# Causal mask of the prompt attention added by TensorE, scores read in PSUM by VectorE and ScalarE

## The reference

```python
def mla_scores(q_lat, q_rope, ckv, krope):
    s = jnp.einsum('bthc,bsc->bhts', q_lat, ckv) + jnp.einsum('bthr,bsr->bhts', q_rope, krope)
    return s.astype(jnp.float32) * SM_SCALE

def mla_prompt(q_lat, q_rope, ckv, krope):
    ...
    def blk(i):
        start = i * Q_BLOCK
        ...
        s = mla_scores(ql, qr, ckv, krope)
        qpos = start + jnp.arange(Q_BLOCK)
        s = jnp.where(kpos[None, :] <= qpos[:, None], s, -jnp.inf)
        p = jax.nn.softmax(s, axis=-1).astype(ckv.dtype)
        return jnp.einsum('bhts,bsc->bthc', p, ckv)
```

## Time and profile before

| | |
|---|---|
| time, median of 3 runs | 1596.08 us (1591.57 to 1596.08) |
| the profiled execution's own time | 1595.94 us |
| its span | 1594.4 us |
| TensorE busy | 1478.6 us (93%) |
| VectorE busy | 694.9 us (44%) |
| ScalarE busy | 457.0 us (29%) |
| chain that ended last, by engine | TensorE 87%, VectorE 8%, DMA 2% |

### The profile page before, as it was taken

How to read it: one execution, slowest core, us unless ns; L and a number is a source line. 1 busy time by engine, 2 the same in 40 slices (tenths; PEclk the granted TensorE clock), 3 DMA queues, 4 the chain that set the end, 5 groups by cost and what they waited for, 6 DMA issues and landing times.

```text
span 1594.4 us, 30443 instructions
## 1 busy us (share of the span) xinstructions
PE 1478.6 (93%) x11990; PEld 1373.2 (86%) x11990; DVE 694.9 (44%) x1155; ACT 457.0 (29%) x774; POOL 144.7 (9%) x275
## 2 busy tenths in 40 slices
PE   5999999999688899999998899988789999999993
PEld 5999999999578888878788878767779999999993
DVE  5444444222565443444343445455474444442224
ACT  4222222222323232333332321223332222222220
POOL 0000000000030015353540000000000000000000
PEclk9999999999778999999999889997879999999996
DMA  3222222322064327575754222132312222223211
GB/s 125 91 92 81 90 92 87 107 91 86 14 233 144 113 81 207 168 206 160 209 162 153 92 93 92 57 109 93 123 42 91 91 81 91 91 90 101 88 67 57
DMA packets 80225, 173.06 MB, mean 109 GB/s; under 512 B 11961, under 2 KB 46778, under 8 KB 78458
## 3 DMA queue, kind: packets, MB, share of 16 engines
q1 hardware_dynamic: 69882, 150.68, 28.7%
q0 software_dynamic: 10240, 20.99, 4.6%
HBM read 157.55 MB, written 14.07 MB: 108 GB/s over the span
## 4 chain that ended last, share of the span: by engine, by line
PE 87%; DVE 8%; DMA 2%; issue 1%; ACT 1%; SPq 0%; DVEq 0%; ACTq 0%
PE acc L559 51%; PE acc L654 15%; PE acc L784 2%; PE acc L781 2%; PE bank_a L744 1%; PE bank_a L745 1%; PE bank_a L724 1%; PE bank_v L927 1%; PE bank_v L759 1%; PE bank_v L903 1%; PE acc L811 1%; PE bank_v L912 1%; DVE rpost L1441 1%; PE bank_a L607 1%; DVE x_lo L1425 1%
## 5 line engine op out<-in xcount | busy, mean ns | idle before, releaser
L559 PE MATMUL acc<-x_hi,w_hi 128*128 128x272 f32 x1536 | 323.5, 292 | 33.1 <-DVE x_lo L1425 29.6
L1400 DVE TENSOR_TENSOR w_lo<-w_raw,w_hi 128x1024 fp32r<-128x1024 f32 (+1 forms) x172 | 223.5, 1300 | 229.4 <-ACT w_hi L1014 225.7
L559 PE MATMUL acc<-x_hi,w_lo 128*128 128x272 f32 x1536 | 319.4, 290 | 0.0
L559 PE MATMUL acc<-x_lo,w_hi 128*128 128x272 f32 x1536 | 319.4, 290 | 0.0
L559 PEld LDWEIGHTS acc<-x_hi,w_hi 128*128 128x128 f32 x1536 | 242.8, 191 | 37.4 <-issue 23.7
L1014 ACT ACTIVATE w_hi<-w_raw 128x1024 fp32r<-128x1024 f32 (+1 forms) x172 | 190.9, 1110 | 199.5 <-PE acc L654 89.2
L559 PEld LDWEIGHTS acc<-x_lo,w_hi 128*128 128x128 f32 x1536 | 244.2, 191 | 0.0
L559 PEld LDWEIGHTS acc<-x_hi,w_lo 128*128 128x128 f32 x1536 | 242.8, 191 | 0.0
L654 PE MATMUL acc<-x_hi,w_hi 128*128 128x272 f32 x688 | 218.8, 318 | 16.2 <-DVE qk L1524 9.2
L654 PE MATMUL acc<-x_hi,w_lo 128*128 128x272 f32 x688 | 205.1, 298 | 0.0
L654 PE MATMUL acc<-x_lo,w_hi 128*128 128x272 f32 x688 | 204.7, 298 | 0.0
(11 more groups left out here) (267 smaller groups left out, 1540.1 us busy)
## 6 DMA issues: line engine op xcount, KB each, us to landing
w_raw<-in_w_gu SPq DMA_DIRECT2D x88, 512.0 KB, 3.4
w_raw<-in_w_dn SPq DMA_DIRECT2D x32, 704.0 KB, 4.0
w_raw<-in_w_in SPq DMA_DIRECT2D x44, 512.0 KB, 4.4
pg<-in_key_t POOLq DMA_DIRECT2D x128, 96.0 KB, 2.5
pg<-in_key_t SPq DMA_DIRECT2D x128, 96.0 KB, 2.2
pg<-in_lat POOLq DMA_DIRECT2D x128, 64.0 KB, 2.6
pg<-in_lat SPq DMA_DIRECT2D x128, 64.0 KB, 2.4
g_mid<-sq SPq DMA_DIRECT2D x16, 272.0 KB, 3.8
```

Of the source, the lines that this page charges most:

```text
L559: ins = nc.tensor.matmul(acc[pair][:, a, 0:HT], w[:, slot, n * P:(n + 1) * P], v[:, k, a * HT:(a + 1) * HT], start=first and n == 0 and te ...
L1400: nc.vector.tensor_tensor(wlo[:, slot, 0:tiles * P], raw[:, slot, 0:tiles * P], f32(whi[:, slot, 0:tiles * P]), ALU.subtract).then_inc(w_s ...
```

## The change

TensorE adds the mask to the scores with a third product in the same accumulation group: the identity matrix times the mask, 128 by 128, onto the last 128 columns of the block. VectorE takes the maximum straight from the PSUM bank, and ScalarE takes the exponential from the bank and writes it to `pr`. The copy `take` and VectorE's mask addition are gone. The bank is now freed by `expo`, which from the second head on also waits for the transposes of the head before, since it overwrites `pr`. In all three programs the dense call behind the scores, 18 products, is cut in two of 9, the first of which now stands between block 2 and block 3. VectorE does `normalise(h, 1)` before `highest(h, 3)`.

```diff
--- before.py
+++ after.py
@@ -310,7 +310,7 @@
         small_out = sem("small_out")
         g1_landed, g2_landed, g1_used, merged = sem("g1_landed"), [sem(f"g2_landed{i}") for i in range(2)], sem("g1_used"), sem("merged")
         pair_landed, qr_ready, qs_done = sem("pair_landed"), sem("qr_ready"), sem("qs_done")
-        mx_ready, ex_ready, inv_ready, pr_ready = sem("mx_ready"), sem("ex_ready"), sem("inv_ready"), sem("pr_ready")
+        mx_ready, pr_ready = sem("mx_ready"), sem("pr_ready")
         ptab_landed, wuv_landed = sem("ptab_landed"), sem("wuv_landed")
         pg_landed = [[[sem(f"pg_landed{w}{b}{q}") for q in range(4)] for b in range(2)] for w in ("sp", "pool")]
         pg_used = sem("pg_used")
@@ -743,7 +743,8 @@
                 b = bank_a(f"sc{h}{i}")
                 nc.tensor.matmul(b[:, 0:n], ql[:, e, i * P:n], ckvT[:, 0:n], start=True, stop=False)
                 nc.tensor.matmul(b[:, 0:n], qr[ROPE * e:ROPE * (e + 1), i * P:n], krT[ROPE * e:ROPE * (e + 1), 0:n],
-                                 start=False, stop=True).then_inc(a_ready, 1)
+                                 start=False, stop=False)
+                nc.tensor.matmul(b[:, i * P:n], ident, mask_qk, start=False, stop=True).then_inc(a_ready, 1)
 
             def turn(h, i):
 
@@ -845,8 +846,9 @@
                     scores(h, 1)
                     sample_scores(m0, (2, 3))
                     scores(h, 2)
+                    dense(9)
                     scores(h, 3)
-                    dense(18)
+                    dense(9)
                     sample_turn(m0)
                     turn(h, 0)
                     turn(h, 1)
@@ -1199,16 +1201,13 @@
             def piece(i):
                 return pr[:, PR_AT[i]:PR_AT[i] + (i + 1) * P]
 
-            def take(h, i):
-
-                act.wait_ge(a_ready, A.filled(f"sc{h}{i}"))
-                nc.scalar.activation(piece(i), A.bank(f"sc{h}{i}")[:, 0:(i + 1) * P], ACT.Copy).then_inc(a_read, 1)
-
             def expo(h, i):
 
                 act.wait_ge(mx_ready, 4 * h + i + 1)
-                nc.scalar.activation(piece(i), piece(i), ACT.Exp, scale=SM,
-                                     bias=sst[:, 4 + i:5 + i], accum_out=sst[:, 8 + i:9 + i]).then_inc(ex_ready, 1)
+                if h:
+                    act.wait_ge(a_ready, A.filled(f"tr{h - 1}{i}"))
+                nc.scalar.activation(piece(i), A.bank(f"sc{h}{i}")[:, 0:(i + 1) * P], ACT.Exp, scale=SM,
+                                     bias=sst[:, 4 + i:5 + i], accum_out=sst[:, 8 + i:9 + i]).then_inc(a_read, 1)
 
             def turned(h, i):
 
@@ -1256,16 +1255,13 @@
                     sample_new(PER * (p // 2))
                 for h in (2 * p, 2 * p + 1):
                     m0, m1 = step_of(2 * h), step_of(2 * h + 1)
-                    take(h, 0)
-                    take(h, 1)
                     expo(h, 0)
                     expo(h, 1)
-                    take(h, 2)
-                    take(h, 3)
                     sample_exp(m0)
                     expo(h, 2)
+                    dense(9)
                     expo(h, 3)
-                    dense(18)
+                    dense(9)
                     sample_turned(m0)
                     turned(h, 0)
                     turned(h, 1)
@@ -1663,15 +1659,13 @@
 
             def highest(h, i):
 
+                dve.wait_ge(a_ready, A.filled(f"sc{h}{i}"))
+                link(nc.vector.reduce_max(sst[:, i:i + 1], A.bank(f"sc{h}{i}")[:, 0:(i + 1) * P], AX.X))
+                nc.vector.tensor_scalar(sst[:, 4 + i:5 + i], sst[:, i:i + 1], -SM, None, ALU.mult).then_inc(mx_ready, 1)
+
+            def normalise(h, i):
+
                 dve.wait_ge(a_read, A.taken(f"sc{h}{i}"))
-                d = piece(i)[:, i * P:(i + 1) * P]
-                link(nc.vector.tensor_tensor(d, d, mask_qk, ALU.add))
-                link(nc.vector.reduce_max(sst[:, i:i + 1], piece(i), AX.X))
-                nc.vector.tensor_scalar(sst[:, 4 + i:5 + i], sst[:, i:i + 1], -SM, None, ALU.mult).then_inc(mx_ready, 1)
-
-            def normalise(h, i):
-
-                dve.wait_ge(ex_ready, 4 * h + i + 1)
                 link(nc.vector.reciprocal(sst[:, 12 + i:13 + i], sst[:, 8 + i:9 + i]))
                 nc.vector.tensor_scalar(piece(i), piece(i), sst[:, 12 + i:13 + i], None, ALU.mult).then_inc(pr_ready, 1)
 
@@ -1750,9 +1744,10 @@
                     sample_highest(m0)
                     normalise(h, 0)
                     highest(h, 2)
+                    normalise(h, 1)
+                    dense(9)
                     highest(h, 3)
-                    normalise(h, 1)
-                    dense(18)
+                    dense(9)
                     normalise(h, 2)
                     normalise(h, 3)
                     dense(18)
```

More of the change, by code:

```diff
@@ L1664, in highest @@
             def highest(h, i):
-                dve.wait_ge(a_read, A.taken(f"sc{h}{i}"))
-                d = piece(i)[:, i * P:(i + 1) * P]
-                link(nc.vector.tensor_tensor(d, d, mask_qk, ALU.add))
-                link(nc.vector.reduce_max(sst[:, i:i + 1], piece(i), AX.X))
+                dve.wait_ge(a_ready, A.filled(f"sc{h}{i}"))
+                link(nc.vector.reduce_max(sst[:, i:i + 1], A.bank(f"sc{h}{i}")[:, 0:(i + 1) * P], AX.X))
                 nc.vector.tensor_scalar(sst[:, 4 + i:5 + i], sst[:, i:i + 1], -SM, None, ALU.mult).then_inc(mx_ready, 1)
             def normalise(h, i):
-                dve.wait_ge(ex_ready, 4 * h + i + 1)
+                dve.wait_ge(a_read, A.taken(f"sc{h}{i}"))
                 link(nc.vector.reciprocal(sst[:, 12 + i:13 + i], sst[:, 8 + i:9 + i]))
```

## The result

| | before | with the change |
|---|---|---|
| time, median of 6 runs | 1593.14 us (1591.06 to 1596.08) | 1603.32 us (1601.0 to 1611.69) |
| ratio | | 1.0073, 95% interval 1.0049 to 1.0096 |
| span of the profiled execution | 1594.4 us | 1599.5 us |
| stretch of the heads, first score product to last transpose (L827, now L828) | 286.6 us | 298.6 us |
| all behind that stretch | 735.3 us | 728.8 us |

The account below looks back on a forecast made before the run. TensorE was taken to bound the heads, so removed work gains 0 us. Added terms 13.3 + 1.6 + 1.2 = 16.1 us on 1595.9 us gave 1612.0 us, 1.0% slower, range 1604 to 1622 us.

Parts of the forecast that it names:

- What bounds the heads: Heads: TensorE busy 298.5 of 299 us, the others wait for it; removing their work gains at most 0.5 us.
- The mask's products: In the eight heads, 32 added fp32 products on TensorE at 0.415 us each: 13.3 us.
- The cut of the dense call: Nine dense products between blocks 2 and 3 add one fp32/dense change each way per head: 1.6 us, between 0 and 2.
- The wait of `turn(h, 1)`: Second transposes wait for block 3's exponential: 0.15 us per head, 1.2 us in all, between 0 and 3.
- theory A: From the experiments: a 128-column product costs TensorE 0.21 us, each change of array shape between neighbours 0.2 us more.
- `scores(h, 2)`, `scores(h, 3)`, `turn(h, 0)`: no wait: In each head, these three places have enough TensorE work as cover while the bank is freed: 0 us.
- Heads 0 and 7, with the weight split between the blocks: Weight split before block 3's maximum and exponential is covered: 0 us, up to 0.5 us in each head if not.
- Maximum in PSUM as fast as in SBUF: VectorE's maximum of 512 columns in the heads takes 0.69 us from either memory.
- The cheap product: Rival: mask product as cheap as a transpose, 0.08 us each, 2.6 us for 32, 1599 us total; 5%.
- The longer hold of the banks: Rival: banks held longer, say 1 us per head at the second transposes, 7 us more, 1619 us; 8%.
- No clock under 1.00: Rival: TensorE's clock dips in the heads, every head 1652 us, 5%; one or two dips 1617 to 1622 us, 10%.
- The rival of dips that move behind the heads: Clock dips after the heads vanish, some 10 us together, giving 1602 us; 7% for one or both, 2% for more.

Follow-up runs that it names:

- copy_gone: Kernel before with only the copy removed, VectorE adding the mask in the PSUM bank, dense call whole: heads 286.6 us, median 1590.9 us, ratio 0.9986.
- two_masks: Changed kernel with the mask product issued twice in each block: heads 305.5 us, median 1611.1 us, ratio 1.011 to the kernel before.
- keys_padded: Kernel before with the rotary part of the scores contracting over 128 rows, keys padded with zeros: heads 276.9 us, median 1585.38 us, ratio 0.9953.
- mask_second: Changed kernel with the mask product between the latent and rotary parts: heads 295.4 us, median 1604.61 us, ratio 1.0064 to the kernel before.

## Why the prediction was right, and where it was off

The forecast was 16.1 us slower, 1.0%; the ratio says 0.73% (0.49 to 0.96), and the stretch of the heads 12.0 us. The median of 1603.32 us lies just under the low end of 1604; part of that is that the before of the same runs is 1593.14 and not the 1595.9 us from which I counted. As a ratio, the range was 1.005 to 1.016 and holds the result. So direction, place and order of size were right, but no added term was: the largest was too big by 4.6 us, the second too big by 1.6 us and the third too small by 2.1 us. That the last two nearly cancel is luck. By its steps:

- **What bounds the heads.** Right, and shown: copy_gone takes 11.5 us off ScalarE and nothing off the time. The bound of 0.5 us for a gain holds.
- **The mask's products: 13.3 us forecast, 8.7 us measured.** The largest miss. The step that failed is "I take the value of the products because the mask's is one of them". The pair of 0.42 us in the earlier trace rows is 0.21 us for the product (a third of the 0.64 us between the pairs of 512 and of 128 columns) and 0.2 us for a change of the array's shape, and in the rows that I read every product had such a change at its side: 32-column loads before block 0, 64 rows in every second product. I saw that "about 0.2 us of each pair doesn't depend on the columns" and took it for a cost of each product. The mask brings 32 products and only eight new changes, in block 1: 32 x 0.213 + 8 x 0.2 = 8.4 us, 0.3 us short of what was measured.
- **The cut of the dense call: 1.6 us forecast, 0.0 measured.** The step that failed is "Each head gets one more change in each direction". The first dense product behind the scores does take longer. But the cut also takes a neighbour away, the mask's product ahead of a latent product, and that gives the same back; the price of the other direction was read from transposes behind dense products, which the cut doesn't add.
- **The wait of `turn(h, 1)`: 1.2 us forecast, 3.3 measured.** Right in place and mechanism, too small by more than half. In head 1 the cover from TensorE's next product on is 1.75 us (614.74 to 616.38, and 0.11 us for one transpose), against 1.76 forecast. The chain is 0.28 us until VectorE starts, 0.73 us for the maximum, 0.19 us, 0.58 + 0.19 us for the exponential and its row sum, and 0.15 us back to TensorE: 2.12 us against 1.91 forecast. Nearly all of the difference is the first term, 0.28 and not 0.11 us, which was read where a block ends with the rotary part. That TensorE's next product starts before the results of the last one are out, because its load goes ahead, fits theory A; no run takes it by itself.
- **`scores(h, 2)`, `scores(h, 3)`, `turn(h, 0)`: no wait.** Right; no line of them stands in the waits.
- **Heads 0 and 7, with the weight split between the blocks: 0 forecast, 0.1 us in each measured.** The low part of the weights holds VectorE until the maximum of block 3 starts, 0.39 us after TensorE's next product (582.56 to 582.95) and not 0.28 as in the six other heads, and the second transposes start 0.56 us and not 0.47 us behind the first. That is 0.2 of the 3.3 us, well within the 0.5 us allowed for each head.
- **Maximum in PSUM as fast as in SBUF.** Right: 0.68 us for 512 columns, against 0.69.
- **The rivals.** The cheap product (0.08 us) is out: 0.217 us in two_masks. That price is between that rival and my own, and my range had both ends. The longer hold of the banks lies between, too: 0.41 us per head, against 0.15 us forecast and 1 us in the rival. No clock under 1.00 stands in the heads. The rival of dips that move behind the heads is half right: in the profiled execution they gave back 6.5 us, but the fit has that as something that goes up and down in every execution of every kernel, before included, and not as an effect of the change.

Of the signs named ahead, three were off: the mask's pair takes 0.25 to 0.32 us and not 0.41 to 0.42, the stretch is longer by 12.0 us and not by 15 to 17, and ScalarE's busy time fell by 11.7 us and not by 14; why the last is less than the time of the copies stays open.

The sum with the measured terms: 8.7 + 0.0 + 3.3 = 12.0 us, the whole difference of the stretch.

## What to carry to other kernels

Where one engine has no idle moment, work taken from the others is worth nothing, and a few percent of work given to it comes back in full; read the stretch, not the span. Take the cost of a wait from the starts of the products around it, against a kernel without the wait, and not from the idle time in a view: here 1.8 us of idle time stood for 3.3 us. Read the price of a product from a row whose neighbours have the same shape as those it will have: here half of what a row showed was the change of shape, not the product. Where products of 64 rows and of 128 rows alternate, zeros in the unused rows can be cheaper than the short product: it took 0.5% off this kernel.

## What the runs showed of the hardware that I had not expected

- An fp32 product with a 128x128 stationary operand holds TensorE for 0.22 us at 128 columns if its neighbours have the same shape, at the clock of 1.00 (two_masks). Between products with 128 and with 64 rows (keys_padded), or with 128 and 32 columns (mask_second), 0.2 us are added; the load of the stationary operand then starts with its product instead of 0.11 us ahead of it.
- A rotary product over 128 rows, half of them zeros, is 0.2 us faster than the same over 64 rows between 128-row neighbours.
- VectorE starts on a block 0.11 us after TensorE's next product begins where the block ends with the 64-row product, and 0.28 us after it where it ends with the mask's product.
- Over 118 executions a microsecond at 1.2 GHz costs this kernel 0.34 us and not 0.5. That TensorE would wait in part of that time anyway is a guess that no run tests.
